# First block of a two-block transformer: six gather buffers instead of eight, and two weight chunks kept from tile 0 to tile 1

## The reference

```python
def peer_ffn(h, wq, subkeys, u, v):
    q = (hf @ wq).reshape(T, PEER_HEADS, 2, D_HALF)
    s = jnp.einsum('thpd,pnd->thpn', q, subkeys, preferred_element_type=jnp.float32)
    ...
    expert = (i1 * N_KEYS + i2).reshape(T, PEER_HEADS * PEER_TOPK)
    ...
    def expert_block(args):
        hc, ec, gc = args
        uc = jnp.take(u, ec, axis=0)
        a = jnp.einsum('cd,ced->ce', hc, uc)
        act = jax.nn.gelu(a, approximate=False) * gc
        vc = jnp.take(v, ec, axis=0)
        return jnp.einsum('ce,ced->cd', act, vc)
```

## Time and profile before

| | |
|---|---|
| median of three runs | 2496.17 us (2494.92 to 2498.85) |
| the profiled execution | 2498.57 us, span 2496.6 us, mean granted TensorE clock 0.939 |
| busy, share of the span | PE 86%, DVE 50%, ACT 31%, POOL 40% |
| moved by DMA | 879.71 MB, mean 352 GB/s |
| first gather issued | 180.46 us |
| last slot added by PE | about 1654.7 us |

### The profile page before, as it was taken

The page is one execution under the profiler, slowest core; times in us unless marked ns, Lnnn a source line. Parts: engine busy times, 40 slices in busy tenths (PEclk is TensorE's granted clock), DMA queues, the critical chain, the costliest instruction groups (busy, mean ns, idle before and its releaser), DMA issues. The chain is left out here.

```text
span 2496.6 us, 28174 instructions
## 1 busy us (share of the span) xinstructions
PE 2135.1 (86%) x8852; PEld 1105.7 (44%) x8852; DVE 1236.8 (50%) x2846; ACT 781.2 (31%) x2244; POOL 1003.1 (40%) x1111
## 2 busy tenths in 40 slices
PE   6988988778888878798978789779889998979997
PEld 2444554233343434445534234246555446645543
DVE  1246589875555485576684864443322222432222
ACT  2233334333435333453343353324110002411001
POOL 1005666676667556676667677720010000000000
PEclk8998999899999989999999899999889999979999
DMA  9979999999999999999999999973269994327996
GB/s 375 364 272 410 404 407 399 409 406 409 407 406 409 404 368 405 385 390 406 405 409 405 407 409 409 409 273 135 101 267 418 417 390 148 123 101 321 418 417 274
DMA packets 237150, 879.71 MB, mean 352 GB/s; under 512 B 23432, under 2 KB 30088, under 8 KB 214496
## 3 DMA queue, kind: packets, MB, share of 16 engines
q0 software_dynamic: 149648, 544.01, 55.1%
q1 hardware_dynamic: 87376, 334.20, 33.9%
HBM read 877.07 MB, written 1.05 MB: 352 GB/s over the span
## 5 line engine op out<-in xcount | busy, mean ns | idle before, releaser
L2289 DVE CUSTOM_DVE_ANT_0 arena<-arena,PS 128x1024 f32<-128x1024 f32 x512 | 624.9, 1221 | 497.3 <-DMA arena<-in_peer_u_dram,IDX 472.1
L966 POOL DMA_INDIRECT arena<-in_peer_v_dram,IDX x512 | 486.6, 950 | 307.8 <-PE PS L1592 185.5
L1592 PE MATMUL PS<-arena,JK 128*128 128x512 f32 x1024 | 505.6, 631 | 115.1 <-ACT JK L1127 112.6
L1592 PE MATMUL PS<-arena 128*128 128x512 f32 x1024 | 509.6, 636 | 109.1 <-ACT arena L1127 94.2
L963 POOL DMA_INDIRECT arena<-in_peer_u_dram,IDX x512 | 488.0, 953 | 239.5 <-issue 127.5
L1592 PEld LDWEIGHTS PS<-arena 128*128 128x128 f32 x1024 | 194.9, 203 | 370.3 <-issue 342.4
L1592 PEld LDWEIGHTS PS<-arena,JK 128*128 128x128 f32 x1024 | 191.2, 199 | 378.7 <-issue 350.7
L1114 ACT ACTIVATE ACTV<-DOT 128x1 f32<-128x1 f32 x512 | 102.8, 201 | 750.7 <-DVE DOT L2289 750.3
L2007 PE MATMUL PS<-arena,HT 128*64 128x256 f32 x2048 | 237.9, 385 | 19.3 <-DMA arena<-in_w_down_dram 12.8
L2007 PEld LDWEIGHTS PS<-arena,HT 128*64 128x64 f32 x2048 | 149.3, 138 | 99.0 <-DMA arena<-in_w_down_dram 22.1
L1122 ACT ACTIVATE GACT<-ACTV,GATE 128x1 f32<-128x1 f32 x512 | 150.9, 295 | 21.1 <-DVE GATE L2277 3.4
(11 more groups left out here) (367 smaller groups left out, 1956.8 us busy)
## 6 DMA issues: line engine op xcount, KB each, us to landing
arena<-in_w_gate_dram SPq DMA_DIRECT2D x64, 1024.0 KB, 16.5
arena<-in_w_up_dram SPq DMA_DIRECT2D x64, 1024.0 KB, 18.6
arena<-in_w_down_dram SPq DMA_DIRECT2D x64, 1024.0 KB, 15.0
arena<-in_w_ada_dram SPq DMA_DIRECT2D x16, 2048.0 KB, 12.1
arena<-in_w_in_dram SPq DMA_DIRECT2D x11, 2048.0 KB, 19.6
arena<-in_peer_wq_dram SPq DMA_DIRECT2D x10, 2048.0 KB, 19.6
mod<-in_w_ada_dram SPq DMA_DIRECT2D x8, 2048.0 KB, 9.1
arena<-in_w_out_dram SPq DMA_DIRECT2D x6, 2048.0 KB, 18.3
```

Source lines behind the costliest of these rows:

```text
L966: pool.indirect_dma_start(out=GV[b], out_offset=None, in_=v_rows, in_offset=off).then_inc(v_loaded[b], 16)
L1592: last = pe.matmul(PO[:, half, :], DIAG[n % DIAGS], GV[BUF[n]][:, half * 512:(half + 1) * 512], start=(j == 0), stop=False, skip_group_che ...
L2289: dve.tensor_tensor_reduce(GU[BUF[n]], GU[BUF[n]], HP[tt].rearrange("p b n -> p (b n)"), 1.0, 0.0, ALU.mult, ALU.add, DOT[:, s:s + 1]).the ...
```

## The change

Before, `RING` (8) gather buffers, two of them in slot 1 of the weight ring. After, six (`GATHERS`) from the first slot to the last, and slot 1 is a place for weights throughout the first block. It takes `("in", 1, 0)`, loaded once and kept from layer 1's tile 0 to tile 1, and then `("wq", 1, 2)`, loaded once and kept in the same way. The other chunks of layer 1 pass through slots 0, 2 and 6 in a new order. In the second block, `("bin", 0, 1)`, which goes to slot 1, no longer waits for the last slot that used buffers 6 and 7 (slot 505), but for slot 509; `("bin", 0, 2)` in slot 3 waits for slot 509 instead of 511. `RING` stays 8 for the small columns.

```diff
@@ -334,11 +334,10 @@
-    (("in", 1, 0, 0), 0), (("in", 1, 1, 0), 2), (("in", 1, 2, 0), 6),
-    (("out", 1, 0, 0), 0), (("out", 1, 1, 0), 2), (("wq", 1, 0, 0), 0), (("wq", 1, 1, 0), 2),
-    (("in", 1, 0, 1), 0), (("in", 1, 1, 1), 2), (("in", 1, 2, 1), 6),
-    (("wq", 1, 2, 0), 0), (("out", 1, 0, 1), 2), (("out", 1, 1, 1), 0), (("wq", 1, 3), 2),
-    (("wq", 1, 0, 1), 0), (("wq", 1, 1, 1), 2), (("wq", 1, 2, 1), 0),
+    (("in", 1, 0), 1), (("in", 1, 1, 0), 0), (("in", 1, 2, 0), 6),
+    (("out", 1, 0, 0), 2), (("out", 1, 1, 0), 0), (("wq", 1, 0, 0), 2), (("wq", 1, 1, 0), 0),
+    (("in", 1, 1, 1), 2), (("in", 1, 2, 1), 6), (("out", 1, 0, 1), 0),
+    (("wq", 1, 2), 1), (("out", 1, 1, 1), 2), (("wq", 1, 3), 0), (("wq", 1, 0, 1), 2), (("wq", 1, 1, 1), 0),
 ]
@@ -348,9 +347,14 @@
-GIVEN_BACK = FIRST_GIVEN_BACK + [name for name, _ in CHUNKS if name not in FIRST_GIVEN_BACK]
+HELD = [("in", 1, 0), ("wq", 1, 2)]
+NEXT_GIVEN_BACK = [name for name, _ in CHUNKS if name not in FIRST_GIVEN_BACK and name not in HELD]
+NEXT_GIVEN_BACK.insert(NEXT_GIVEN_BACK.index(("in", 1, 1, 1)), HELD[0])
+NEXT_GIVEN_BACK.insert(NEXT_GIVEN_BACK.index(("wq", 1, 1, 1)) + 1, HELD[1])
+GIVEN_BACK = FIRST_GIVEN_BACK + NEXT_GIVEN_BACK
 NSLOT = 8
-PAIR_SLOTS = (3, 1)
+PAIR_SLOTS = (3,)
+GATHERS = 6
@@ -370,8 +374,7 @@
-    order = [0, 1, 2, 3, 4, 5] * 4
-    order += [(6 + n) % RING for n in range(DEPTH * TT * SLOTS - len(order))]
+    order = [n % GATHERS for n in range(DEPTH * TT * SLOTS)]
@@ -383,7 +386,7 @@
-    return (kind, l, c) if l == 0 or (kind, c) == ("wq", NQ - 1) else (kind, l, c, tt)
+    return (kind, l, c) if l == 0 or (kind, l, c) in HELD or (kind, c) == ("wq", NQ - 1) else (kind, l, c, tt)
@@ -788,10 +791,12 @@
-                for b in range(2):
-                    if name == ("bin", 0, 2 - b):
-
-                        sp.wait_ge(expert_added, max(n for n in range(len(BUF)) if BUF[n] // 2 == 2 + b) + 1)
+                if name == ("bin", 0, 1):
+
+                    sp.wait_ge(expert_added, len(BUF) - 2)
+                if name == ("bin", 0, 2):
+
+                    sp.wait_ge(expert_added, max(n for n in range(len(BUF)) if BUF[n] // 2 == 2) + 1)
```

More of the change, by code:

```diff
@@ L502, in pair @@
             return ring[PAIR_SLOTS[b // 2 - 2]][:, at:at + D]
-        GU, GV = ([pair(b, which) for b in range(RING)] for which in range(2))
+        GU, GV = ([pair(b, which) for b in range(GATHERS)] for which in range(2))
         DIAG = [tile[:, n * P:(n + 1) * P] for tile in (gv(8192, 512), JKT[:]) for n in range(DIAGS // 2)]
@@ L599, in build @@
         h_in_psum = sem("h_in_psum")
-        u_loaded = [sem(f"u_loaded{i}") for i in range(RING)]
-        v_loaded = [sem(f"v_loaded{i}") for i in range(RING)]
+        u_loaded = [sem(f"u_loaded{i}") for i in range(GATHERS)]
+        v_loaded = [sem(f"v_loaded{i}") for i in range(GATHERS)]
         dot_ready = sem("dot_ready")
@@ L770, in _ @@
                     sp.dma_start(NGAIN[0][1], row(norm2_g[0], P)).then_inc(gains_loaded, 16)
-                if name == ("in", 1, 0, 0):
+                if name == ("in", 1, 0):
                     arrived(sp, ("h2T", 0, 1, 1))
```

## The result

The changed kernel takes 2517.65 us in the median of four runs (2505.97 to 2521.27), beside 2495.55 for the kernel before (2491.34 to 2498.85, four runs). The ratio is 1.0083, 95% interval 1.0051 to 1.0115. Two repetitions, each beside its own runs of the kernel before, gave 1.0104 (1.0087 to 1.0121) and 1.0077 (1.0056 to 1.0098). So the change costs 18 to 24 us. The forecast was +9.0 us, 2505.2, with a range up to 2516: the direction held, the size was off by a factor of 2.0 to 2.6, and the median lies outside the range.

The account below looks back on a forecast made before the run. The first block was taken to last as long as its DMA bytes at 409 GB/s, with few losses from late requests. 19.5 - 1.3 - 5.1 - 4.1 = +9.0 us gave 2505.2 us, range 2489 to 2516.

Parts of the forecast that it names:

- the signs named ahead: What the profile after would show: 875.5 MB, longer waits for PE, emptier stretches, landings of 4.8 to 5.5 us.
- two buffers fewer: First block's gathers: asked for six slots ahead, cover shrinks by 5.1 us, engines run dry: +19.5 us.
- six stretches: First-block stretches where GpSimd waits for PE: losses of 3.7, 3.7, 2.3, 5.1, 2.2 and 2.5 us.
- elsewhere (420 to 860 and after 1300 us): Rest of the first block: queue deeper or waits short, so fewer buffers cost nothing.
- the cap of 5.1: Upper limit on each stretch's loss from fewer buffers: 2 x 2.56 = 5.1 us.
- T: Landing time below which the DMA engines run dry: taken as 5.5 us, between 4.8 and 6.9.
- slower still: Rival: DVE and PE coupled more tightly, engines dry below 6.9 us landings; +16.0 us, 2512, or 2517; chance 0.22.
- Its coupling of DVE and PE: DVE, also only six slots ahead of PE, lengthens the two lossy stretches by a slot each: 5 us more.
- A load moves: Tile 1's output chunks asked for earlier; 5.1 us of transfer moves from second lossy stretch to first: 0, bounds -5.1 and +5.1.
- Loaded once: Layer 1's first input chunk and third query chunk lose their second loads: -1.3 (bounds 0 and 5.1) and -5.1 us.
- The wait: First block's end: second block's load waits for slot 509, so last dot products come 2.56 us apart: -4.1 us.

Follow-up runs that it names:

- e2: Kernel before with six gather buffers from first slot to last, chunks and second block's waits unchanged: 2524.5 us, ratio 1.0113, +28.6 us.
- e5: Kernel before with seven pairs of gather buffers instead of eight; the second block's chunk for slot 1 then waits for slot 507: 2497.46 us, ratio 1.0011.
- e6: Kernel before with six buffers for `peer_u` and eight for `peer_v`, counted apart: 2500.43 us, ratio 1.0016.
- e7: Kernel before with eight buffers for `peer_u` and six for `peer_v`, counted apart: 2520.4 us, ratio 1.0113.
- e13: Changed kernel with only the third routing piece of query chunk 2 moved on DVE, from slot 305 to 313: 2516.11 us, ratio 1.0079.
- e14: Changed kernel with DVE routing pieces before slots 301, 307, 313 and 334, 339, 344: 2513.84 us, ratio 1.0082.
- e15: Changed kernel with the load of `("out", 1, 1, 1)` held back until slot 288 is added: 2509.98 us, ratio 1.0057.
- e3: Kernel before, eight buffers, with the two second loads left out (computes other numbers): 2493.67 us, ratio 0.999.
- e4: Kernel before with only the second block's chunk for slot 1 waiting for slot 509 instead of 505: 2493.55 us, ratio 0.9991.
- e10: Kernel before with seven buffers for `peer_u` and nine for `peer_v` (slots 24 to 503), and bin(0,1) waiting for slot 509: 2485.67 us, ratio 0.9974.
- e11: Kernel before with bin(0,1) waiting for slot 509 and DVE routing pieces of query chunk 2 three slots apart instead of two: 2493.4 us, ratio 0.9992.
- e8: Changed kernel with five buffers for `peer_u` and seven for `peer_v` instead of six each: 2509.29 us, ratio 1.0064.
- e16: Changed kernel with `("out", 1, 1, 1)` held back until slot 288 is added and `("in", 1, 1, 1)` until slot 237 is: 2515.73 us, ratio 1.0075.

## Why the prediction was too low

**What was right.** The mechanism: with six buffers `peer_v`'s gathers are asked for too late while PE is held up, and the DMA engines run dry. Of the signs named ahead, the bytes, the longer waits, the three emptier stretches and the 2.56 us at the end all came. One didn't: the shortest landings were to be 4.8 to 5.5 us in most stretches; one of the six did so (4.8), three went down to 4.1 and 4.2, and two stayed at 6.8 and 7.0. Even 4.1 is above the 3.2 us that we estimated from the Trainium skill's "DMA: Bandwidth & Descriptors" (section on the anatomy of one DMA on the GpSimd path); no gather here landed as fast as that.

**The step that failed is the first term: "two buffers fewer", +19.5 us.** It measured 28.6 (e2). Two sentences of it are wrong: that each of six stretches can lose 5.1 us at most and once, and that "elsewhere (420 to 860 and after 1300 us)" costs nothing. The rows show where. Table of stretches of e2, laid around the same slots as those of before that follow:

```profile
384.00:412.00 28.00, 22.22 (x63) 10.77 (x64) 24.98 (x79) 12.36 (x36) 15.76 (x18) 0.88 0.89 324
500.00:530.00 30.00, 23.00 (x44) 9.49 (x45) 26.38 (x77) 11.26 (x38) 21.41 (x23) 0.87 1.00 380
764.00:784.00 20.00, 18.16 (x48) 8.82 (x48) 9.96 (x18) 9.72 (x31) 12.06 (x14) 0.83 0.97 369
884.00:940.00 56.00, 44.67 (x138) 23.02 (x139) 48.63 (x135) 22.53 (x62) 28.62 (x31) 0.85 0.93 349
1044.00:1092.00 48.00, 39.43 (x149) 24.03 (x150) 27.81 (x74) 20.07 (x61) 22.95 (x25) 0.82 0.89 325
1096.00:1128.00 32.00, 24.14 (x57) 10.17 (x56) 23.82 (x50) 16.43 (x44) 20.12 (x21) 0.89 0.88 341
1192.00:1222.00 30.00, 26.93 (x122) 17.35 (x123) 23.09 (x55) 13.32 (x38) 16.90 (x18) 0.90 0.93 342
1256.00:1284.00 28.00, 21.05 (x62) 10.47 (x61) 26.02 (x74) 12.36 (x34) 14.69 (x15) 0.88 0.96 359
1300.00:1316.00 16.00, 12.47 (x24) 4.99 (x24) 14.40 (x29) 7.59 (x20) 11.27 (x12) 0.89 0.97 359
1444.00:1484.00 40.00, 32.50 (x65) 13.41 (x66) 31.78 (x92) 16.97 (x51) 28.36 (x33) 0.88 1.01 374
```

The kernel before, at the places where it isn't full, and at the one where e2 has a second spell:

```profile
384.00:412.00 28.00, 23.59 (x70) 11.41 (x71) 26.29 (x81) 12.12 (x35) 15.99 (x17) 0.88 1.01 391
880.00:936.00 56.00, 46.92 (x145) 24.08 (x146) 50.17 (x139) 24.00 (x68) 29.46 (x33) 0.88 0.97 364
1032.00:1084.00 52.00, 42.49 (x173) 26.84 (x174) 37.60 (x98) 22.20 (x69) 27.32 (x29) 0.84 0.97 358
1088.00:1118.00 30.00, 28.89 (x74) 12.76 (x73) 19.50 (x40) 18.07 (x48) 22.81 (x24) 1.00 1.03 410
```

Each row is read as in the prediction: length x (1 - GB/s / 409) is the time in which nothing was moved. At the other six places before has 407 to 409 GB/s, at most 0.2 us each.

| place (slots) | predicted | before | e2 | lost |
|---|---|---|---|---|
| 384 (60 to 70) | 3.7 | 1.2 | 5.8 | 4.6 |
| 884 (237 to 255) | 3.7 | 6.2 | 8.2 | 2.0 |
| 960 to 1020 | 2.3 | 0.6 | 0.6 | 0 |
| 1044 (288 to 303) | 5.1 | 6.5 | 9.9 | 3.4 |
| 1096 (304 to 316) | with the last | 0 | 5.3 | 5.3 |
| 1192 (about 333) | 2.2 | 0.1 | 4.9 | 4.8 |
| 1256 (about 354) | 2.5 | 0 | 3.4 | 3.4 |
| 500, 764, 1300, 1444 | 0 | 0.3 | 9.5 | 9.2 |
| sum | 19.5 | 14.9 | 47.6 | 32.7 |

32.7 stands beside the 30.8 us by which the slots end later. The two kernels move the same bytes, so the sums had to come near each other; what the rows tell is where the time goes. Of the 13.2 us above the forecast, 9.2 lie in the places costed at nothing, and 3.6 come from there being two spells, at 1044 and 1096 us, where one was priced; the other places together are off by 0.4. No single place loses more than 5.3; the cap of 5.1 was about right for one spell, and the count of spells was wrong. From 1044 to 1128 us there are two of them. The second is not there before at all, and by the timelines it is made by the first: gathers late by the hold up (1029.7 to 1044.3 us before, from slot 288's add to slot 289's) leave DVE with routing still to do when PE adds slots in 1.72 us each and catches up; dot product 305 is late, so its add, so `peer_v`'s gather six slots on, before which GpSimd stands for 5.39 us. No run took the first spell away alone to show it. Timelines of DVE and of GpSimd in e2 (the idle time's releaser is given as "issue"; the add it waited for, slot 305's, ends at 1109.0):

```profile
1102.26 0.18 DVE L2261 TENSOR_SCALAR IDX<-arena 128x32 int32<-128x32 f32 x1
1102.35 0.18 DVE L2263 TENSOR_TENSOR GATE<-arena 128x32 f32<-128x32 f32 x1
1102.85 1.22 DVE L2288 CUSTOM_DVE_ANT_0 arena<-arena,PS 128x1024 f32<-128x1024 f32 x1 [0.31 <-DVE GATE L2263]
```

```profile
1110.67 1.20 POOL L965 DMA_INDIRECT arena<-in_peer_v_dram,IDX  x1 [5.39 <-issue]
```

In the kernel before the same dot product starts at 1084.51 us and PE comes to it at 1088.8: it had the time. The four places "elsewhere" were written off because landings there were long. Long median landings say that the queue is deep on the average, not that it stays so when one add is late. Nor is there one T for the rule: what was lost at 384, 884 and 1192 us (4.6, 2.0 and 4.8, beside shortest landings of 6.9, 6.9 and 8.4) would need T at 6.4, 3.8 and 8.1 us. That the six losses came to 19.5 at 5.5 is a choice within that spread.

Why the second buffer costs so much more than the first (some 23 us of slots after 8) stays open. e5 and e2 show that it does, and e6 and e7 that the two together cost what they do on `peer_v`'s side. A possible reading, which no run tests, is that most hold ups are shorter than the cover of seven slots (17.9 us at 2.56) and longer than that of six (15.4). The rival "slower still" was nearest in time, 2512 to 2517, and its 26.5 for the buffers lies near the 28.6, but that is luck: it puts them on the same six stretches, 3.7 of them on 960 to 1020 us, where nothing was lost. Its coupling of DVE and PE was not confirmed either: e13 and e14 moved the jumps and not the sum.

**"A load moves": 0, bounds -5.1 and +5.1.** At its own two spells the profile gives about the upper bound for each, and at a later place something back that the prediction didn't price. Table of stretches of the changed kernel:

```profile
884.00:940.00 56.00, 46.39 (x140) 24.22 (x141) 48.02 (x135) 21.71 (x60) 28.95 (x31) 0.83 0.86 315
1048.00:1096.00 48.00, 38.41 (x158) 24.36 (x158) 29.97 (x82) 20.36 (x63) 23.19 (x25) 0.86 0.80 284
1264.00:1300.00 36.00, 22.51 (x44) 8.75 (x44) 29.32 (x89) 12.98 (x37) 23.23 (x24) 0.90 1.03 403
```

56 x (1 - 315/409) = 12.9 us empty against 8.2 in e2, and 14.7 against 9.9: 4.7 and 4.8 us more, a chunk each (307 and 309, 283 and 282 GB/s in the changed kernel's other two profiles). The second spell lost the load of 1053 us to places that were full. The first gets as many bytes as before, but no longer the load at 891, just ahead of its driest 10 us (890 to 900, 156 GB/s). The prediction gave both stretches spare time "of about that size" and left out that a load is worth something only at the instant when the engines run dry; e15's filled spell (6.5 us less empty) shows that much, what it is worth in time is not shown. The other way, 1264 has 0.5 us empty for e2's 3.4, and about as little in the other two profiles: there the second block's first two chunks now come, asked for at 1258.8 us, since their places are free 85 us earlier than before (1343.8). The second spell, at 1104 us, has 3.2 us empty for e2's 5.3 in this profile, but 5.0 and 5.2 in the other two, so nothing came back there.

**"Loaded once": -1.3 and -5.1.** Together 6.4 were forecast and 2.3 measured (e3), with eight buffers, not clear of nothing. The first saves nothing there (the 6.8 us above): of its bounds, 0 was right. How much of the query chunk's 5.1 is saved is not shown: e3's slots gain 6.2 us on the kernel before between slots 350 and 420, but those of e6, which loads everything, lose 4.2 on it there, and nothing in e6's edit explains that.

**The wait: -4.1.** The last three slots gain 4.1 us in each profile with it, as forecast; the median gains 2.4 (e4), the slots' end 2.6.

**The sum.** Each part by itself: 28.6 (e2) - 2.3 (e3) - 2.4 (e4) = +23.9, beside 22.1, 23.8 and 17.8 for the whole change, measured three times. The first term's error, 9.1 us, is the larger part of the miss. The forecast of the savings, 10.5, is less certain: e3 and e4 find 4.7 with eight buffers, the medians of e2 and of the changed kernel lie 5 to 12 us apart, and the slots' ends 9 to 12. The measurements don't settle it.

## What to carry to other kernels

Where a ring of buffers covers an engine's hold ups, ask which wait holds each side of it and size the sides apart: one half megabyte moved from the side with slack to the one without, with one later wait, gained 8 us (e10), and two taken from the side without slack cost 25 (e7). Count hold ups, not stretches, and look at a second one behind each, since the first uses up the lead that hides the second; and don't extrapolate from the first buffer taken away to the next. A load that "costs" 5 us of bandwidth can cost nothing while it fills a dry spell (leaving the first of e3's out left the engines idle 6.8 us longer), so taking it away or moving it is to be priced by what the engines would do at that instant.

## What the hardware showed

The second block has the same instructions in every kernel, yet it takes from the slots' end 842.0 us in the kernel before, 842.7 in e2, 842.9 in e11, but 830.8 and 831.1 in two profiles of the changed kernel and 835.6 in the third. The granted clock goes with it: over the whole second block it is 0.95 in the profiles of 831 us, 0.94 in those of 836 (the changed kernel's third, e8, e10) and 0.93 in those of 838 to 843. The second block of the kernel before and of the changed kernel:

```profile
1655.00:2496.00 841.00, 753.21 (x4400) 444.20 (x4400) 247.16 (x567) 153.38 (x398) 8.71 (x17) 0.93 0.67 267
```

```profile
1674.00:2504.00 830.00, 738.71 (x4400) 431.77 (x4400) 246.03 (x566) 153.42 (x398) 8.70 (x17) 0.95 0.69 274
```

And 92 us of each, from 92 us behind the slots' end:

```profile
1746.00:1838.00 92.00, 74.45 (x310) 49.71 (x312) 31.35 (x87) 18.08 (x40) 6.78 (x11) 0.74 0.26 98
```

```profile
1765.00:1857.00 92.00, 73.92 (x363) 46.11 (x364) 31.55 (x87) 17.05 (x35) 6.77 (x11) 0.83 0.35 126
```

PEclk 0.74 or 0.83 (a share of the time at 2.4 GHz and the rest at 1.2) and 310 or 363 matmuls in the same time. When in the second block the low level is granted differs between executions, by 4.9 us in the three profiles of the changed kernel and by 12.5 over all profiles (830.8 to 843.3, the latter in e16). It is the likely reason why the profiled execution of the changed kernel (2505.97, mean clock 0.946, the others 0.937 to 0.940) lies below its median by 11.7 us, and why the twelve runs of e10 fall into two groups, seven of 2483 to 2486.5 us (clock 0.943 to 0.945) and five of 2490.6 to 2494.3 (0.936 to 0.943). For effects under 10 us it helps to look at the slots' end beside the median, though one profile each leaves some 3 us open.
